# FFN modulation vectors: the partial sum is split into a rounded half and a remainder, and spread by two matmuls in the rounded format

## The chip, the core and the metric

The kernel runs on one core of a Trainium2 chip. The core has a matrix engine (TensorE, PE in the rows), a vector engine (VectorE, DVE), an engine for activations and copies (ScalarE, ACT), a general one (GpSimd, POOL) and a queue engine (SyncE, SP). They run side by side and meet only at semaphores. The metric is the device time of one execution in microseconds (us), lower is better; each version is timed in several runs and the median counts.

## What is computed

Two decoder layers on a sequence of 256 tokens with 1024 features. Each layer has two gated FFNs and a mixer between them, and a vector projected from the conditioning input `c` shifts, scales and gates each of them:

```
def reference(x, c, ada_w, ada_b, ...):
    h = x
    c_act = jax.nn.silu(c)
    for i in range(DEPTH):                                  # DEPTH = 2
        mod = c_act @ ada_w[i] + ada_b[i]                   # 1024 x 9216
        sh1, sc1, gt1, sh2, sc2, gt2, sh3, sc3, gt3 = jnp.split(mod, N_MOD, axis=-1)
        h = h + 0.5 * gt1 * swiglu(modulate(h, sh1, sc1), ffn_w_gu[i, 0], ffn_w_down[i, 0])
        u = modulate(h, sh2, sc2)
        m = dsa_mixer(u, ...) if i % 2 == 0 else rwkv7_mixer(u, ...)
        h = h + gt2 * m
        h = h + 0.5 * gt3 * swiglu(modulate(h, sh3, sc3), ffn_w_gu[i, 1], ffn_w_down[i, 1])
    return h
```

`swiglu(x, w_gu, w_down)` is `(silu(x @ gate) * (x @ up)) @ w_down` with 2816 hidden features. The change concerns `mod` alone, and of it the parts that are computed during the FFNs.

## The kernel before

**FFNs.** Every large matrix is used in two parts: a part rounded to the format fp32r (`_hi`, a copy on ACT) and the remainder (`_lo`, a subtraction on DVE). A product is then three matmuls, hi by hi, lo by hi and hi by lo (lines 662 to 664, whatever the matrices). There are four FFNs; I number them 0 to 3. Each runs 11 blocks of 256 hidden features (function `ffn` on each engine; `run_blocks` writes out the first three and the last ones and loops over the others). In block b PE does, in this order: gate and up products of the first 128 tokens (24 matmuls, `gate_up`), the transposes of the previous block's hidden values, the down products of the previous block for the first 128 tokens (12 matmuls, `down(ub - 1, 0)`), the gate and up products of the other 128 tokens, transposes, and `down(ub - 1, 1)`. The order on each engine is written by hand; nothing is scheduled. `down(ub - 1, 0)` waits for `split[2]`, the remainder of the down weights (DVE line 1506, `rest_of_down`), which itself waits for their rounding (ACT line 1112, `round_down`). That rounding waits for the end of `down(ub - 2, 1)`, since the rounded weights have one buffer. After the last block comes a tail in which both `down` calls stand together.

**Modulation vectors.** `mod` is made in 36 pieces of 512 columns, numbered v. Four are made at the start, three in the first mixer (DSA), the others in FFNs 0 to 2: 11, 11 and 7 pieces (`ADA_FFN`), one in each block while there are any. FFN 3 makes none. For a piece DVE does eight multiply-and-add steps over `ada_raw` (line 1433, `ada_products`), each 128x512, into `ada_acc`: this leaves 128 partial sums per column. These stand at the end of DVE's work for a block. In the next block PE sums them over the partitions, and at the same time spreads the sum to all 128 partitions, by one matmul with a matrix of ones in full fp32 (`ada_total`, line 635). It stands between the transposes and `down(ub - 1, 0)`. ACT copies the result to `mods` (line 1097). The weights come by DMAs that ACT issues (`load_ada`, lines 1087 and 1092), right behind `round_down` in its order.

ACT's order in a block from b = 1 on is: `silu` and `round_hidden` of the previous block, `round_down`, `load_ada`, `round_block` (two casts of the next gate and up weights, `gu_hi`), `silu`, `round_hidden`, `copy_mods`. DVE's is: `times_up`, `rest_of_hidden`, `rest_of_down`, `rest_of_block` (`gu_lo`), `times_up`, `rest_of_hidden`, `ada_products`. In the tail ACT does `silu`, `round_hidden(last, 0)`, `round_down`, `round_hidden(last, 1)`, and in FFNs 0 to 2 also the `round_block` of the next phase; DVE does `times_up`, `rest_of_hidden(last, 0)`, `rest_of_down`, `rest_of_hidden(last, 1)`, the next phase's `rest_of_block` and the residual. Each engine takes its instructions in order, so a wait holds all that stands behind it.

Of the kernel before, what the change touches and what calls it, by code (L numbers as in the profile page):

```python
# [5 lines left out]
P = 128  # L6
F32 = mybir.dt.float32
# [9 lines left out]
def trunk(nc, a, out):  # L17
# [37 lines left out]
    HALF = 512  # L55
# [9 lines left out]
    ON_PE = 2  # L65
    ADA_FFN = ((4, NB), (18, NB), (29, 7), (36, 0))

    ctx = ExitStack()
    with ctx:
# [67 lines left out]
        front_bias = place("front_bias", [P, ADA_FRONT, HALF], at=ada_at)  # L137
        front_acc = [ada_acc[:], hid[:].rearrange("p t c -> p (t c)")]
        c_wide = place("c_wide", [P, 2, P], at=spare_at)

# [81 lines left out]
        front_in = [[sem(f"front_in_{j}_{i}") for i in range(4)] for j in range(ADA_FRONT)]  # L222
        front_bias_in = sem("front_bias_in")
        front_step = sem("front_step")
        c_wide_ready = sem("c_wide_ready")
        ada_step = sem("ada_step")
        ada_sum = sem("ada_sum")
        mods_ready = sem("mods_ready")
        g_ready = [sem("g_ready_0"), sem("g_ready_1")]
# [184 lines left out]
        def _(sp):  # L414
# [3 lines left out]
            sp.dma_start(front_bias[0:1, :, :].rearrange("p v n -> p (v n)"), a["ada_b"][0:1, 0:ADA_FRONT * HALF]  # L418
                         ).then_inc(front_bias_in, 16)

# [210 lines left out]
        def _(pe):  # L631
# [14 lines left out]
            def front_total(j):  # L646

                pe.wait_ge(front_step, (j + 1) * (KD - ON_PE))
                nc.tensor.matmul(TB[j % 2][:], ones[:], front_acc[j % 2], start=False, stop=True).then_inc(ada_sum, 1)

            def turn_x(q, parts=range(4)):

                for i in parts:
                    pe.wait_ge(xn_ready, 4 * q + i + 1)
                    for k in range(4):
                        mm = nc.tensor.transpose(bank[4 + i][:, k * P:(k + 1) * P], xn[:, i % 2, k * P:(k + 1) * P],  # L656
                                                 ident[:])
                    mm.then_inc(xn_turned, 1)
# [55 lines left out]
            def ffn(f, q):  # L714
# [9 lines left out]
                def step(b, odd, ada):  # L724
# [6 lines left out]
                    if not (peeled and b == 0):  # L731
                        turn_hidden(ub - 1, 1, peeled and ub == 1)
                        if nv and not (peeled and b > nv):
                            pe.wait_ge(hT_ready[0], ub)
                            ada_total(v0 + b - 1, TB[0])
                        down(ub - 1, 0, peeled and b == 1, False)
                        pe.wait_ge(hid_ready[1], ub)
                    elif f:
                        pe.wait_ge(xT_ready, turned + 4)
# [14 lines left out]
                if nv == NB:  # L754
                    ada_total(v0 + NB - 1, TB[0])

# [310 lines left out]
            pe.wait_ge(consts, 5)  # L1067
            pe.wait_ge(c_wide_ready, 1)
            for j in range(3):
# [11 lines left out]
        def _(act):  # L1081
            def load_ada(v, layer, hv, first=False):
# [6 lines left out]
                for i in range(4):  # L1089
                    if not first:  # L1090
                        act.wait_ge(ada_step, done + 2 * i - 6)
                    act.dma_start(ada_raw[:, i], ada_w[layer, :, 2 * i:2 * i + 2, bass.ds(hv * HALF, HALF)]
                                  ).then_inc(ada_in[i], 16)

            def copy_mods(v, hv, spread):
# [254 lines left out]
            def ffn(f, q=None):  # L1350
# [30 lines left out]
                if f < 3:  # L1381

                    round_block(n0 + NB, (n0 + NB) % 2, width=DSA_SMALL if f == 0 else HALF)
                if nv == NB:
                    copy_mods(v0 + NB - 1, v0 % HV + NB - 1, TB[0])

            act.wait_ge(c_in, 16)
            nc.scalar.activation(cact[:], ccol[:], ACT.Silu).then_inc(c_ready, 1)
            nc.scalar.activation(c_wide[:], ccol[:, 0:ON_PE].unsqueeze(2).broadcast_to([P, ON_PE, P]), ACT.Silu
                                 ).then_inc(c_wide_ready, 1)  # L1390
            act.wait_ge(consts, 5)
            copy_mods(0, FRONT[0][0], TB[0])
            squares_of_h(0)
# [20 lines left out]
        def _(dve):  # L1414
# [55 lines left out]
            def first_modulate():  # L1470

                dve.wait_ge(front_bias_in, 16)
                front_products(0)
# [18 lines left out]
                rest_of_first_x(2)  # L1492
                rest_of_first_x(3)

            def rest_of_block(n, par, width=HALF, buf=raw, halves=range(2)):
# [246 lines left out]
            def ffn(f, q):  # L1742
# [194 lines left out]
```

## Time and profile before

| what | value |
|---|---|
| median of 3 runs | 1535.7 us (1533.28 to 1538.37) |
| the profiled execution | 1535.84 us, of which span 1534.1 us |
| PE matmul busy | 1297.3 us, 85% of the span |
| DVE busy | 957.4 us, 62% |
| ACT busy | 527.8 us, 34% |
| POOL busy | 79.3 us, 5% |
| the chain that ended last | PE 73%, DVE 16%, ACT 4%, DMA 3%, issue 2%, SP queue 2% |
| the same by line | lines 662, 664, 663: 19% each |
| `ada_total` (line 635) | 32.7 us busy, 64 records of 593 ns |
| `ada_products` (line 1433) | 168.4 and 23.8 us busy |

The time is the span plus 1.7 us around it. The program prints a line number per instruction; a helper such as `products` has one number for all its uses, so what tells the uses apart are the names of the tiles. The clock column is the TensorE clock that was granted, 1.00 for 2.4 GHz and 0.50 for 1.2 GHz. FFN 0 runs from about 42 to 257 us, FFN 1 from 471 to 683, FFN 2 from 687 to 900 and FFN 3 from 1326 to the end.

### The profile page before, as it was taken

The numbers are of one execution on the slowest core, as the hardware profiler recorded it, in microseconds if no ns is written. First come the engines' busy times: TensorE is split into PE (matmuls) and PEld (weight loads), VectorE is DVE, ScalarE is ACT, GpSimd is POOL, SyncE is SP. The second block draws the span as 40 slices with busy tenths as digits, with TensorE's granted clock in tenths as the row PEclk, the third lists the DMA queues.
The fourth block names the chain that finished last, engine by engine and source line by source line (L and its number), as shares of the span: only waits on it lengthen the run. The fifth ranks groups of instructions, "written<-read, shape, count | busy, mean of one in ns | idle before, by whom it ended". The sixth has DMA issues, their size and how long they took to land.

```text
span 1534.1 us, 16872 instructions
## 1 busy us (share of the span) xinstructions
PE 1297.3 (85%) x6370; PEld 1033.1 (67%) x6370; DVE 957.4 (62%) x1232; ACT 527.8 (34%) x694; POOL 79.3 (5%) x67
## 2 busy tenths in 40 slices
PE   5899996975988999979999938776746995899997
PEld 2678884763566888857788824675735994688885
DVE  6697776767457887768785364356592338645543
ACT  2433432353324333434443234343411011344331
POOL 1000000000000000000000000005260004000000
PEclk9899998885578999989999967888756555899998
DMA  9788874730017888668886442310102012455641
GB/s 315 281 297 286 278 253 162 254 129 1 0 60 256 297 303 289 224 214 270 296 303 208 79 127 91 115 56 0 28 0 56 2 56 91 137 184 167 208 146 55
DMA packets 186515, 252.19 MB, mean 164 GB/s; under 512 B 31506, under 2 KB 122642, under 8 KB 186450
## 3 DMA queue, kind: packets, MB, share of 16 engines
q1 hardware_dynamic: 151570, 184.14, 36.1%
q10 hardware_dynamic: 34880, 67.18, 12.7%
q8 instruction: 42, 0.69, 0.2%
q14 instruction: 23, 0.18, 0.0%
HBM read 249.19 MB, written 2.10 MB: 164 GB/s over the span
## 4 chain that ended last, share of the span: by engine, by line
PE 73%; DVE 16%; ACT 4%; DMA 3%; issue 2%; SPq 2%; ACTq 0%; POOL 0%; DVEq 0%; POOLq 0%
PE bank L662 19%; PE bank L664 19%; PE bank L663 19%; DVE inv_tmp L1670 2%; PE bank L814 2%; PE bank L635 2%; PE bank L1029 1%; PE bank L1037 1%; DVE gu_lo L1500 1%; PE bank L700 1%; PE bank L824 1%; DVE inv_out L1672 1%; PE bank L846 1%; PE bank L983 1%; DVE xn L1543 1%
## 5 line engine op out<-in xcount | busy, mean ns | idle before, releaser
L662 PE MATMUL bank<-gu_hi,xT_hi 128*128 128x512 f32 (+1 forms) x880 | 354.8, 403 | 17.0 <-ACT z L1169 8.4
L663 PE MATMUL bank<-gu_lo,xT_hi 128*128 128x512 f32 (+1 forms) x880 | 352.0, 400 | 0.0
L664 PE MATMUL bank<-gu_hi,xT_lo 128*128 128x512 f32 (+1 forms) x880 | 351.7, 400 | 0.0
L1500 DVE TENSOR_TENSOR gu_lo<-raw,gu_hi 128x2048 fp32r<-128x2048 f32 (+1 forms) x116 | 257.2, 2255 | 82.7 <-ACT gu_hi L1105 82.5
L1105 ACT CAST gu_hi<-raw 128x2048 fp32r<-128x2048 f32 (+1 forms) x116 | 213.3, 1883 | 82.0 <-PE bank L664 29.8
L662 PEld LDWEIGHTS bank<-gu_hi,xT_hi 128*128 128x128 f32 x880 | 172.9, 196 | 58.0 <-ACT z L1169 9.3
L663 PEld LDWEIGHTS bank<-gu_lo,xT_hi 128*128 128x128 f32 x880 | 172.8, 196 | 38.1 <-issue 1.0
L664 PEld LDWEIGHTS bank<-gu_hi,xT_lo 128*128 128x128 f32 x880 | 172.3, 196 | 36.1
L1506 DVE TENSOR_TENSOR dn_lo<-raw,dn_hi 128x2048 fp32r<-128x2048 f32 x44 | 100.8, 2291 | 123.2 <-ACT dn_hi L1112 123.2
L1433 DVE SCALAR_TENSOR_TENSOR ada_acc<-ada_raw,cact,ada_acc 128x512 f32<-128x512 f32 x224 | 168.4, 752 | 12.0 <-DVE ada_acc L1433 1.0
L662 PE MATMUL bank<-dn_hi,hT_hi 128*128 128x512 f32 x352 | 156.7, 445 | 17.9 <-DVE dn_lo L1506 17.9
L1119 ACT ACTIVATE hid<-bank 128x256 f32<-128x256 f32 x88 | 33.4, 381 | 317.9 <-PE bank L664 317.9
L664 PE MATMUL bank<-dn_hi,hT_lo 128*128 128x512 f32 x352 | 142.0, 403 | 0.0
L663 PE MATMUL bank<-dn_lo,hT_hi 128*128 128x512 f32 x352 | 141.6, 402 | 0.0
L1112 ACT CAST dn_hi<-raw 128x2048 fp32r<-128x2048 f32 x44 | 83.8, 1905 | 94.4 <-PE bank L664 94.4
L1511 DVE TENSOR_TENSOR hid<-hid,bank 128x256 f32<-128x256 f32 x88 | 36.6, 416 | 93.3 <-ACT hid L1119 93.3
L662 PEld LDWEIGHTS bank<-dn_hi,hT_hi 128*128 128x128 f32 x352 | 68.6, 195 | 38.6 <-issue 26.4
L663 PEld LDWEIGHTS bank<-dn_lo,hT_hi 128*128 128x128 f32 x352 | 68.7, 195 | 18.0 <-issue 5.7
L664 PEld LDWEIGHTS bank<-dn_hi,hT_lo 128*128 128x128 f32 x352 | 68.5, 195 | 15.7
L656 PE MATMUL bank<-ident,xn 128*128 128x128 f32 x96 | 24.7, 407 | 45.3 <-DVE xn L1543 44.1
L662 PE MATMUL bank<-xT_hi,gu_hi 128*128 128x256 f32 x128 | 38.7, 303 | 20.6 <-DVE xT_lo L1592 18.9
L656 PEld LDWEIGHTS bank<-ident,xn 128*128 128x128 f32 x96 | 16.0, 202 | 55.5 <-DVE xn L1543 53.0
(255 smaller groups left out, 1571.3 us busy)
## 6 DMA issues: line engine op xcount, KB each, us to landing
raw<-in_ffn_w_gu_dram SPq DMA_DIRECT2D x176, 512.0 KB, 6.3
ada_raw<-in_ada_w_dram ACTq DMA_DIRECT2D x128, 512.0 KB, 5.5
raw<-in_ffn_w_down_dram SPq DMA_DIRECT2D x44, 1024.0 KB, 6.9
raw<-in_rwkv_w_rkv_dram SPq DMA_DIRECT2D x24, 512.0 KB, 5.5
front<-in_ada_w_dram SPq DMA_DIRECT2D x16, 512.0 KB, 10.2
raw<-in_dsa_w_in_dram SPq DMA_DIRECT2D x16, 512.0 KB, 6.1
raw<-in_dsa_w_out_dram SPq DMA_DIRECT2D x8, 512.0 KB, 5.4
out_raw<-in_rwkv_w_out_dram SPq DMA_DIRECT2D x4, 512.0 KB, 5.4
```

Source lines behind the costliest of these rows:

```text
L635: nc.tensor.matmul(spread[:], ones[:], ada_acc[:], start=True, stop=True).then_inc(ada_sum, 1)
L656: mm = nc.tensor.transpose(bank[4 + i][:, k * P:(k + 1) * P], xn[:, i % 2, k * P:(k + 1) * P], ident[:])
L662: nc.tensor.matmul(out_ap, sta_hi, mov_hi, start=start, stop=False, skip_group_check=True)
L663: nc.tensor.matmul(out_ap, sta_hi, mov_lo, start=False, stop=False, skip_group_check=True)
L664: return nc.tensor.matmul(out_ap, sta_lo, mov_hi, start=False, stop=stop, skip_group_check=True)
L1105: nc.scalar.copy(gu_hi[:, par, 4 * i:4 * i + 4, 0:width], buf[:, i, 0:4 * width].rearrange("p (k c) -> p k c", k=4)).then_inc(hi_ready[i], 1)
L1112: nc.scalar.copy(dn_hi[:], raw[:, 2, :].rearrange("p (t d) -> p t d", t=2)).then_inc(hi_ready[2], 1)
L1119: nc.scalar.activation(hid[:, half, :], G[half][:, 0:FB], ACT.Silu).then_inc(silu_done[half], 1)
L1433: nc.vector.scalar_tensor_tensor(out=ada_acc[:], in0=ada_raw[:, k // 2, k % 2, :], scalar=cact[:, k:k + 1], in1=ada_acc[:] if k else ada_b ...
L1500: nc.vector.tensor_tensor(gu_lo[:, par, ks, 0:width], buf[:, i, 0:4 * width].rearrange("p (k c) -> p k c", k=4), gu_hi[:, par, ks, 0:width ...
L1506: nc.vector.tensor_tensor(dn_lo[:], raw[:, 2, :].rearrange("p (t d) -> p t d", t=2), dn_hi[:].bitcast(F32), ALU.subtract).then_inc(split[2 ...
L1511: nc.vector.tensor_tensor(hid[:, half, :], hid[:, half, :], G[half][:, FB:2 * FB], ALU.mult).then_inc(hid_ready[half], 1)
```

## The change

The change makes the sum over partitions in the rounded format too, in the FFNs alone. For each of the 29 pieces made in FFNs 0 to 2:

- ACT gets a copy `acc_hi` <- `ada_acc` that rounds to fp32r (`round_acc`), placed between `round_hidden` and `round_down`; it waits for the eighth product step.
- DVE gets a subtraction `acc_lo` <- `ada_acc` - `acc_hi` (`rest_of_acc`), between `rest_of_hidden` and `rest_of_down`; it waits for `acc_hi`.
- PE's fp32 matmul becomes two fp32r matmuls with rounded ones, over `acc_hi` and `acc_lo` (`ffn_total`), and waits for `acc_lo`.
- In the tails of FFNs 0 and 1 `round_acc` stands on ACT behind the next phase's `round_block`, while `rest_of_acc` stands on DVE ahead of `rest_of_down`.
- At the start ACT makes the rounded ones; the semaphores for `c` and for the first biases are joined, and so are those for what ACT makes of `c`. So ACT's first activation waits for the biases too.

The three pieces in DSA and the four at the start keep the fp32 matmul.

```
@@ PE
+            def ffn_total(f, b):
+                u = ADA_DONE[f] + b
+                pe.wait_ge(acc_ready, u + 1)
+                nc.tensor.matmul(TB[0][:], ones_r[:], acc_hi[:], start=True, stop=False)
+                nc.tensor.matmul(TB[0][:], ones_r[:], acc_lo[:], start=False, stop=True).then_inc(ada_sum, 1)
...
                             pe.wait_ge(hT_ready[0], ub)
-                            ada_total(v0 + b - 1, TB[0])
+                            ffn_total(f, b - 1)
...
@@ ACT
+            def round_acc(v):
+                act.wait_ge(ada_step, (v - ADA_FRONT) * KD + KD)
+                nc.scalar.copy(acc_hi[:], ada_acc[:]).then_inc(acc_hi_ready, 1)
...
                         round_hidden(ub - 1, 0, peeled and ub == 1)
+                        if nv and not (peeled and b > nv):
+                            round_acc(v0 + b - 1)
                         round_down(ub - 1, peeled and ub == 1)
...
                     round_block(n0 + NB, (n0 + NB) % 2, width=DSA_SMALL if f == 0 else HALF)
                 if nv == NB:
+                    round_acc(v0 + NB - 1)
                     copy_mods(v0 + NB - 1, v0 % HV + NB - 1, TB[0])
-            act.wait_ge(c_in, 16)
+            act.wait_ge(c_in, 2 * 16)
...
+            nc.scalar.copy(ones_r[:], ones[:]).then_inc(c_ready, 1)
...
@@ DVE
+            def rest_of_acc(f, b):
+                dve.wait_ge(acc_hi_ready, ADA_DONE[f] + b + 1)
+                nc.vector.tensor_tensor(acc_lo[:], ada_acc[:], acc_hi[:].bitcast(F32), ALU.subtract).then_inc(acc_ready, 1)
...
                         rest_of_hidden(ub - 1, 0)
+                        if nv and not (peeled and b > nv):
+                            rest_of_acc(f, b - 1)
                         rest_of_down(ub - 1)
...
                 rest_of_hidden(last, 0)
+                if nv == NB:
+                    rest_of_acc(f, NB - 1)
                 rest_of_down(last)
```

ACT's queue at the tail of FFN 1 and the start of FFN 2, after the change (`dn_hi` is the rounded down weights, `gu_hi` the rounded gate and up weights, `hT_hi` the rounded hidden values):

```order
L1127 CAST dn_hi<-raw 128x2048
L1140 CAST hT_hi<-bank 128x256
L1120 CAST gu_hi<-raw 128x2048 x2
L1108 CAST acc_hi<-ada_acc 128x512
L1112 COPY mods<-bank 128x512
```

Before, the same place had all of these but the `acc_hi` line, which now stands behind both `gu_hi` casts.

ACT's queue in block 1 of an FFN, after the change:

```order
L1140 CAST hT_hi<-bank 128x256
L1108 CAST acc_hi<-ada_acc 128x512
L1127 CAST dn_hi<-raw 128x2048
L1098 DMA ada_bias<-in_ada_b_dram 1x512
L1103 DMA ada_raw<-in_ada_w_dram 128x2x512 x4
L1120 CAST gu_hi<-raw 128x2048 x2
```

Here `acc_hi` came in ahead of `dn_hi`, so the down weights, the DMAs and the `gu_hi` casts all stand behind its wait.

## Rows read from the trace of the kernel before

**Rows 1.** Windows, two whole blocks of FFN 2: with a piece, and without one

```profile
core 0: us, PE busy (x) PEld busy (x) DVE busy (x) ACT busy (x) POOL busy (x), PEclk, DMA share, GB/s
779.80:797.60 17.80, 17.80 (x80) 14.24 (x79) 14.03 (x16) 7.29 (x8) 0.00 (x0) 1.00 0.85 294
831.10:848.05 16.95, 16.95 (x78) 13.87 (x77) 8.12 (x7) 6.78 (x7) 0.00 (x0) 1.00 0.57 186
```

**Rows 2.** Timeline of PE (start us, duration us, what), around one sum in FFN 0

```profile
158.65 1.02 PE L635 MATMUL bank<-ada_acc,ones 128*128 128x512 f32 x2
...
159.74 0.39 PE L663 MATMUL bank<-dn_lo,hT_hi 128*128 128x512 f32 x1
159.97 0.39 PE L664 MATMUL bank<-dn_hi,hT_lo 128*128 128x512 f32 x1
```

**Rows 3.** Timeline of ACT, then of DVE, one steady block of FFN 0

```profile
153.23 1.91 ACT L1112 CAST dn_hi<-raw 128x2048 fp32r<-128x2048 f32 x1 [2.42 <-PE bank L664]
...
171.02 1.90 ACT L1112 CAST dn_hi<-raw 128x2048 fp32r<-128x2048 f32 x1 [2.33 <-PE bank L664]
...
163.97 5.48 DVE L1433 SCALAR_TENSOR_TENSOR ada_acc<-ada_raw,cact,ada_acc 128x512 f32<-128x512 f32 x7
...
172.95 2.29 DVE L1506 TENSOR_TENSOR dn_lo<-raw,dn_hi 128x2048 fp32r<-128x2048 f32 x1 [2.83 <-ACT dn_hi L1112]
```

**Rows 4.** Timeline of ACT and DVE, one cast and one tensor operation of 128x512

```profile
263.86 0.58 ACT L1155 CAST xT_hi<-bank 128x512 fp32r<-128x512 f32 x1 [2.92 <-PE bank L656]
...
677.81 0.69 DVE L1561 TENSOR_TENSOR h<-h,xn 128x512 f32<-128x512 f32 x1
```

**Rows 5.** Timeline of ACT, DVE and PE, block 1 of FFN 0

```profile
59.60 1.90 ACT L1112 CAST dn_hi<-raw 128x2048 fp32r<-128x2048 f32 x1
...
60.78 4.82 DVE L1433 SCALAR_TENSOR_TENSOR ada_acc<-ada_raw,cact,ada_acc 128x512 f32<-128x512 f32 x6 [0.53 <-DVE ada_acc L1433]
...
66.19 2.28 DVE L1506 TENSOR_TENSOR dn_lo<-raw,dn_hi 128x2048 fp32r<-128x2048 f32 x1
...
66.41 1.04 PE L635 MATMUL bank<-ada_acc,ones 128*128 128x512 f32 x2
68.62 0.47 PE L662 MATMUL bank<-dn_hi,hT_hi 128*128 128x512 f32 x1 [1.17 <-DVE dn_lo L1506]
...
78.60 0.41 PE L700 MATMUL bank<-ident,hid 128*128 128x128 f32 x2 [1.53 <-issue]
```

**Rows 6.** Timeline of DVE and PE, block 1 of FFN 1

```profile
488.44 4.04 DVE L1433 SCALAR_TENSOR_TENSOR ada_acc<-ada_raw,cact,ada_acc 128x512 f32<-128x512 f32 x5
...
494.69 1.02 PE L635 MATMUL bank<-ada_acc,ones 128*128 128x512 f32 x2
495.49 0.47 PE L662 MATMUL bank<-dn_hi,hT_hi 128*128 128x512 f32 x1
```

**Rows 7.** Timeline of DVE and PE, block 1 of FFN 2

```profile
702.94 5.68 DVE L1433 SCALAR_TENSOR_TENSOR ada_acc<-ada_raw,cact,ada_acc 128x512 f32<-128x512 f32 x7
...
712.10 1.02 PE L635 MATMUL bank<-ada_acc,ones 128*128 128x512 f32 x2
```

**Rows 8.** Timeline of ACT and PE, tail of FFN 0

```profile
242.11 1.90 ACT L1112 CAST dn_hi<-raw 128x2048 fp32r<-128x2048 f32 x1 [2.33 <-PE bank L664]
...
244.18 0.77 ACT L1105 CAST gu_hi<-raw 128x288 fp32r<-128x288 f32 x2
...
246.48 0.47 PE L662 MATMUL bank<-dn_hi,hT_hi 128*128 128x512 f32 x1 [4.19 <-DVE dn_lo L1506]
```

**Rows 9.** Timeline of ACT, DVE and PE, tail of FFN 1

```profile
669.21 3.70 ACT L1105 CAST gu_hi<-raw 128x2048 fp32r<-128x2048 f32 x2
...
669.07 2.29 DVE L1506 TENSOR_TENSOR dn_lo<-raw,dn_hi 128x2048 fp32r<-128x2048 f32 x1 [3.73 <-ACT dn_hi L1112]
...
677.08 0.69 DVE L1559 SCALAR_TENSOR_TENSOR xn<-bank,mods 128x512 f32<-128x512 f32 x1 [0.99 <-PE bank L664]
...
671.51 0.77 PE L662 MATMUL bank<-dn_hi,hT_hi 128*128 128x512 f32 x1 [4.19 <-DVE dn_lo L1506]
```

**Rows 10.** Timeline of PE behind a pause, then the window that follows

```profile
35.33 0.47 PE L662 MATMUL bank<-gu_hi,xT_hi 128*128 128x512 f32 x1 [3.17 <-DVE gu_lo L1500]
...
35.90:45.80 9.90, 7.80 (x17) 4.93 (x16) 6.76 (x10) 2.38 (x2) 0.00 (x0) 0.50 0.33 106
```

More of the change, by code:

```diff
@@ L66, in trunk @@
     ADA_FFN = ((4, NB), (18, NB), (29, 7), (36, 0))
+    ADA_DONE = tuple(sum(n for _, n in ADA_FFN[:f]) for f in range(4))
     ctx = ExitStack()
@@ L114, in trunk @@
         chunk_decay = place("chunk_decay", [P, KD, NC])
+        ones_r = place("ones_r", [P, P], F32R, at=top["at"])
         rstat = place("rstat", [P, 128])
@@ L138, in trunk @@
         front_acc = [ada_acc[:], hid[:].rearrange("p t c -> p (t c)")]
+        acc_hi = place("acc_hi", [P, HALF], F32R, at=spare_at + 2048)
+        acc_lo = place("acc_lo", [P, HALF], F32R, at=spare_at + 4096)
         c_wide = place("c_wide", [P, 2, P], at=spare_at)
@@ L222, in trunk @@
         front_in = [[sem(f"front_in_{j}_{i}") for i in range(4)] for j in range(ADA_FRONT)]
-        front_bias_in = sem("front_bias_in")
         front_step = sem("front_step")
-        c_wide_ready = sem("c_wide_ready")
         ada_step = sem("ada_step")
         ada_sum = sem("ada_sum")
+        acc_hi_ready = sem("acc_hi_ready")
+        acc_ready = sem("acc_ready")
         mods_ready = sem("mods_ready")
@@ L418, in _ @@
             sp.dma_start(front_bias[0:1, :, :].rearrange("p v n -> p (v n)"), a["ada_b"][0:1, 0:ADA_FRONT * HALF]
-                         ).then_inc(front_bias_in, 16)
+                         ).then_inc(c_in, 16)
             def load_front(j):
@@ L754, in ffn @@
                 if nv == NB:
-                    ada_total(v0 + NB - 1, TB[0])
+                    ffn_total(f, NB - 1)
             def dsa(q):
@@ L1067, in _ @@
             pe.wait_ge(consts, 5)
-            pe.wait_ge(c_wide_ready, 1)
+            pe.wait_ge(c_ready, 3)
             for j in range(3):
@@ L1384, in ffn @@
                 if nv == NB:
+                    round_acc(v0 + NB - 1)
                     copy_mods(v0 + NB - 1, v0 % HV + NB - 1, TB[0])
[L1387 removed]
+            act.wait_ge(c_in, 2 * 16)
             nc.scalar.activation(cact[:], ccol[:], ACT.Silu).then_inc(c_ready, 1)
             nc.scalar.activation(c_wide[:], ccol[:, 0:ON_PE].unsqueeze(2).broadcast_to([P, ON_PE, P]), ACT.Silu
[L1390 removed]
+                                 ).then_inc(c_ready, 1)
             act.wait_ge(consts, 5)
+            nc.scalar.copy(ones_r[:], ones[:]).then_inc(c_ready, 1)
             copy_mods(0, FRONT[0][0], TB[0])
@@ L1470, in first_modulate @@
             def first_modulate():
-                dve.wait_ge(front_bias_in, 16)
+                dve.wait_ge(c_in, 2 * 16)
                 front_products(0)
```

## The prediction

> **What bounds the kernel now.** I read the windows of single blocks first, then the timelines of PE, ACT and DVE side by side where the change puts something. In a block that makes a piece of `mod`, PE is busy for all 17.80 us at full clock, while DVE is busy for 14.03, ACT for 7.29 and the DMA engines 0.85 of the time; in a block without a piece PE is again busy throughout, for 16.95 us [rows 1]. So in the FFN blocks PE sets the pace, and what PE is spared there counts in full, as long as the other engines keep up. At the ends of the FFNs it is different: PE waits 4.19 us there for the remainder of the down weights [rows 8, 9], and in block 1 of FFN 0 it waits 1.17 us for it [rows 5]. There a later `dn_lo` counts in full. The change touches both kinds of place.
>
> **Part 1, the cheaper sum, in steady blocks.** Matmuls of 128x512 in the rounded format follow each other 0.23 us apart (159.74 to 159.97). The record of the first down matmul is stretched, so I count back: the one that starts at 159.74 is the second of its group, its predecessor took a slot from about 159.51, and the fp32 sum had PE from 158.65 to there, 0.86 us [rows 2]. The two windows say the same: 17.80 less 16.95 is 0.85 [rows 1]. Two rounded matmuls are 2 x 0.23 = 0.46, so a block gets 0.40 us shorter. The price in the other direction is certain within little: at best the new pair costs less by a few hundredths, at worst the switch of operands shows and 0.05 is lost.
>
> Do the others keep up? The new cast on ACT needs about 0.58 us and the subtraction on DVE about 0.69 [rows 4]. ACT waits for PE for 2.33 us ahead of `dn_hi` at 171.02. The products end at 163.97 + 5.48 = 169.45, `acc_hi` then takes ACT to about 170.1, nearly a microsecond before it is wanted for `dn_hi`. DVE waits 2.83 us for `dn_hi` [rows 3] and does `acc_lo` inside that. So both are hidden. The ring that could take over is: `dn_hi` starts at 153.23, products end at 169.45, 16.22 us later [rows 3]; with the cast 0.58 and two hand-overs of some 0.05 it is 16.9, against a block of 17.80 - 0.40 = 17.40. PE still sets the pace, by 0.5 us. The DMA share would go from 0.85 to 0.87 [rows 1].
>
> This holds for blocks 2 to 10 of FFNs 0 and 1 and blocks 2 to 7 of FFN 2: 9 + 9 + 6 = 24 blocks, **-9.6 us** (24 x 0.40; bounds -8.4 and -10.6).
>
> **Part 2, block 1 of an FFN.** Here the products are late against ACT, because block 0 has no down work. In FFN 0 ACT started `dn_hi` at 59.60, but the products ended only at 60.78 + 4.82 = 65.60. Now ACT stands at `round_acc` until then: `acc_hi` to 66.2, `dn_hi` (1.90) to 68.1, `dn_lo` (2.28) to 70.4, and `down(0, 0)` starts at about 70.5 and not at 68.62 [rows 5], 1.9 later. Behind it PE used to wait 1.53 us at 78.60 [rows 5], which swallows most: the delay left is 1.9 - 1.5 = 0.4 us. That cover holds if the late ada DMAs behind the cast do no harm. They are issued some 5 us later, which leaves the gate and up weights more of the bandwidth; I see no loss. But PE now stands idle from the end of the sum, about 67.3 with the wait for `acc_lo`, to 70.5: 3.2 us. After a pause of 3.17 us at the start of the program the clock was at 0.50 for the next 9.9 us, after the pauses of 1.17 and 1.53 it was not [rows 10, 5]. What a fall costs: in the tail of FFN 1, behind a pause of 4.19 us, twelve down matmuls took 677.08 - 671.51 = 5.6 us, where twelve at full clock take 2.8; 2.8 lost [rows 9]. At the edge as this pause is, I take a bit more than half of that, 1.6. Term: **+2.0 us** (bounds +0.3 and, from half of the 9.9 us of low clock, +5).
>
> The Trainium skill, "TensorE: Matmul & The Clock Gate", section "HAM oscillation — how this bites in real kernels", has it that a wait between two bursts of matmuls sends the engine back to half rate, so that the burst behind starts cold. By that rule this term is about 2.0; without it, 0.4. The pauses of 3.17 us [rows 10] and 4.19 us [rows 9] agree with it.
>
> In FFN 1 the products end at 488.44 + 4.04 = 492.48. `acc_hi` to 493.1, `dn_hi` to 495.0, `dn_lo` to 497.3: `down` starts at 497.4 against 495.49 [rows 6], and nothing behind it waits. The pause is 495.15 to 497.4, 2.2 us, between rows that kept the clock and a row that lost it; I take it as kept. **+1.9 us** (bounds +1.4 and, with a lost clock, +4.7).
>
> In FFN 2 the products end at 702.94 + 5.68 = 708.62; the same steps give 713.5 for the end of `dn_lo`, while the fp32 sum at 712.10 ended at 712.96 [rows 7]. **+0.5 us** (bounds +0.2 and +1.0). In all three ACT's `gu_hi` gets 1.6 to 2.4 us later as well; PE wants the following `hid` some 7 us after that, so it is covered.
>
> **Part 3, the tails.** In the tail DVE stops at `rest_of_acc` until ACT has made `acc_hi`, and ACT does that only after `hT_hi` and the two `gu_hi` casts of the next phase. In FFN 0 these are narrow: 244.18 + 0.77 = 244.95, `acc_hi` to 245.5, `acc_lo` to 246.15. `dn_lo`, which began right behind `dn_hi` at 244.0, begins at 246.2, and PE starts at 248.6 instead of 246.48 [rows 8]: **+2.2 us** (bounds +2.0 and +4.0, the upper one if the low clock lasts longer over the two `down` calls). In FFN 1 they are full size: 669.21 + 3.70 = 672.9, `acc_hi` to 673.5, `acc_lo` to 674.1, so `dn_lo` starts 5.1 us later than at 669.07 and PE at 676.6 instead of 671.51. The residual at 677.08 waits for that `down` [rows 9] and moves with it: **+5.0 us** (bounds +4.2 and +5.5). The cheaper sums of the tails save nothing, as PE idles for microseconds behind them.
>
> **Part 4, the start.** ACT's first activation now waits for the bias DMA and for one more small cast. The first product waits for weights that land much later. 0.
>
> **Sum.** -9.6 + 2.0 + 1.9 + 0.5 + 2.2 + 5.0 = **+2.0 us**. The profiled execution, 1535.84 us with 1534.1 of span and 1.7 around it, becomes 1537.8; it stands 0.1 above the median, so I predict **1537.7 us**, which is 0.13% more and no change that can be told: about 0.3% (4.6 us) is what a measurement of this kernel can tell from none.
>
> **Rivals.**
> *(a) The clock stays up in block 1 of FFN 0 and the tails overlap a little better.* The pause of 3.2 us is so close to the one row of 3.17 that it may go either way; then part 2 begins with +0.4, the tails cost 2.0 and 4.4. Sum -9.6 + 0.4 + 1.9 + 0.5 + 2.0 + 4.4 = -0.4: **1535.3 us**. Chance 0.22.
> *(b) Slower: the pauses cost clock everywhere.* If block 1 of FFN 0 and block 1 of FFN 1 both lose the 2.8 us of [rows 9] (0.4 + 2.8 = 3.2 and 1.9 + 2.8 = 4.7), and the longer pause lengthens the tail of FFN 0 to 3.9, the sum is -9.6 + 3.2 + 4.7 + 0.5 + 3.9 + 5.0 = +7.7: **1543.4 us**. It decides at a pause of between 1.53 us, which kept the clock [rows 5], and 3.17 us, which lost it [rows 10]. Chance 0.20.
> *(c) Slower: the ring of ACT and DVE takes over.* If the cast and its hand-overs take 1.2 us instead of 0.7, the ring of 16.9 reaches 17.4; at 1.4 it would take 0.2 us back in each of 24 blocks, +4.9: **1542.6 us**. Against it: every hand-over from DVE to ACT and back seen in the rows takes under 0.1 us. Chance 0.05.
> *(d) Faster: the waits of part 3 do not appear,* because ACT gets to `acc_hi` sooner than its order says. Then -9.6 + 2.0 + 1.9 + 0.5 = -5.2: **1530.5 us**. The order on ACT is fixed, so only 0.05.
> The forecast has the remaining 0.48.
>
> **How the numbers follow.** The forecast and rival (a) hold 0.70; to leave out no more than 0.2 the range must go into (b) and (c), and ends at the price of (b). Downwards it takes in (a) with the better bound of part 1 and of block 1 of FFN 1, -0.4 - 1.0 - 0.5 = -1.9, and the 2 us by which single runs differ: 1532. Range **1532 to 1543.5**. Faster by over 0.3% (under 1531.1): (d) and a sliver of (a), 0.07. Slower by over 0.3% (over 1540.3): (b), (c) and the upper end of the forecast, 0.27. Within: 0.66.
>
> **What the profile after would show.** Part 1: blocks 17.4 us apart in the steady part (starts of `dn_lo`), PE without idle time, ACT still waiting for PE ahead of `dn_hi`. Part 2: in block 1 of each FFN an `acc_hi` that starts as the eighth product ends, `dn_hi` behind it, and PE idle ahead of the first down matmul for 3.2, 2.2 and 1.0 us; the clock in the stretch behind tells (a) from the forecast and from (b). Part 3: PE idle in the tails of FFNs 0 and 1 for 6.3 and 9.3 us and not 4.19, DVE waiting for ACT's `acc_hi`; FFN 2 and FFN 3 end as before. The prediction is wrong if steady blocks are 17.6 or longer (a bound that I don't see) or if the idle time of the tails has not grown.

## The result, and the profile after

| | kernel before | kernel after |
|---|---|---|
| median of its runs | 1536.82 us (20 runs, 1533.28 to 1538.37) | 1539.19 us (20 runs, 1536.09 to 1542.13) |
| ratio, 95% interval | | 1.0017 [1.001, 1.0024] |
| profiled execution: span | 1534.1 us | 1537.0 us |
| granted clock, mean | 0.845 | 0.840 |

The change costs 0.17%, some 2.6 us. The interval leaves out 1, so by this many runs the kernel is a little slower. It stays within the 0.3% that the prediction called no change. The median of before has moved from 1535.7 (3 runs) to 1536.82 (20 runs), so 1.1 of the 1.5 us between the 1537.7 predicted and 1539.19 are the starting point and not the change.

The page after says little by itself; busy time per engine and the chain that ended last:

```profile
PE 1283.5 (84%) x6370; PEld 1033.1 (67%) x6370; DVE 977.6 (64%) x1261; ACT 545.4 (35%) x724; POOL 78.5 (5%) x67
...
PE 69%; DVE 18%; ACT 4%; DMA 4%; issue 2%; SPq 2%; ACTq 0%; POOL 0%; DVEq 0%; POOLq 0%
```

PE is most of the chain, and DVE the second. Where they take turns is seen only place by place.

**A steady block.** The window of one whole block of FFN 2 with a piece (columns as in [rows 1]), then the timeline of PE around a sum in FFN 1:

```profile
779.80:797.16 17.36, 17.36 (x80) 14.23 (x79) 14.72 (x17) 7.91 (x9) 0.00 (x0) 1.00 0.88 303
```

```profile
603.34 0.38 PE L711 MATMUL bank<-ident,hid 128*128 128x128 f32 x2
603.47 0.47 PE L659 MATMUL bank<-acc_hi,ones_r 128*128 128x512 f32 x1
603.79 0.40 PE L660 MATMUL bank<-acc_lo,ones_r 128*128 128x512 f32 x1
604.02 0.39 PE L673 MATMUL bank<-dn_hi,hT_hi 128*128 128x512 f32 x1
```

A block takes 17.36 us and not 17.80 [rows 1], 0.44 less, with PE busy in all of it. The four rows of the sum show why: the record at 603.47 is stretched over its predecessor, so I count back one slot of 0.23 from 603.79 to about 603.56; from there to the first down matmul at 604.02 the pair takes 0.46 us, where the fp32 sum took 0.86 [rows 2]. The other engines have 0.69 us (DVE, 14.03 to 14.72) and 0.62 us (ACT, 7.29 to 7.91) more to do.

What ACT and DVE do in such a block of FFN 1:

```profile
580.77 1.91 ACT L1127 CAST dn_hi<-raw 128x2048 fp32r<-128x2048 f32 x1 [0.40 <-PE bank L675]
...
597.12 0.62 ACT L1108 CAST acc_hi<-ada_acc 128x512 fp32r<-128x512 f32 x1 [1.32 <-DVE ada_acc L1452]
598.13 1.90 ACT L1127 CAST dn_hi<-raw 128x2048 fp32r<-128x2048 f32 x1 [0.38 <-PE bank L675]
...
582.71 2.29 DVE L1530 TENSOR_TENSOR dn_lo<-raw,dn_hi 128x2048 fp32r<-128x2048 f32 x1 [1.61 <-ACT dn_hi L1127]
...
591.61 5.48 DVE L1452 SCALAR_TENSOR_TENSOR ada_acc<-ada_raw,cact,ada_acc 128x512 f32<-128x512 f32 x7
```

ACT waits 1.32 us for the eighth product, casts for 0.62, and then still waits 0.38 us for PE ahead of `dn_hi`, where it had waited 2.33 [rows 3]. So ACT comes to the down weights with 0.38 us in hand. DVE waits 1.61 us for `dn_hi`, before 2.83 [rows 3].

**Block 1 of FFN 0**, timeline of ACT, DVE and PE:

```profile
67.20 0.62 ACT L1108 CAST acc_hi<-ada_acc 128x512 fp32r<-128x512 f32 x1 [5.68 <-DVE ada_acc L1452]
67.72 1.90 ACT L1127 CAST dn_hi<-raw 128x2048 fp32r<-128x2048 f32 x1
69.54 3.71 ACT L1120 CAST gu_hi<-raw 128x2048 fp32r<-128x2048 f32 x2
...
62.34 4.82 DVE L1452 SCALAR_TENSOR_TENSOR ada_acc<-ada_raw,cact,ada_acc 128x512 f32<-128x512 f32 x6 [0.53 <-DVE ada_acc L1452]
...
69.66 2.29 DVE L1530 TENSOR_TENSOR dn_lo<-raw,dn_hi 128x2048 fp32r<-128x2048 f32 x1 [1.11 <-ACT dn_hi L1127]
...
72.09 0.47 PE L673 MATMUL bank<-dn_hi,hT_hi 128*128 128x512 f32 x1 [2.53 <-DVE dn_lo L1530]
```

ACT stands for 5.68 us at the cast, until the products end at 62.34 + 4.82 = 67.16, and all that is behind it in its queue stands with it. PE's pause ahead of its first down matmul has grown from 1.17 [rows 5] to 2.53 us. In the profile before, the second half of the weights of block 2 was rounded here, after a wait for its DMA:

```profile
73.94 1.91 ACT L1105 CAST gu_hi<-raw 128x2048 fp32r<-128x2048 f32 x1 [5.92 <-DMA raw<-in_ffn_w_gu_dram]
```

After, both halves run at 69.54 without a wait. The clock behind PE's pause, and behind the pause of 1.86 us in block 1 of FFN 1 (windows, the columns as before; the clock is the third number from the end):

```profile
72.80:76.10 3.30, 3.30 (x9) 2.53 (x9) 3.30 (x2) 1.47 (x4) 0.00 (x0) 0.50 1.05 396
...
500.00:503.40 3.40, 3.40 (x16) 2.77 (x15) 3.40 (x2) 1.97 (x4) 0.00 (x0) 1.00 1.08 331
```

In FFN 0 the clock fell to 0.50, which is 1.2 GHz of the 2.4, for 3.3 us: 9 matmul records where 16 stand in a like window at full clock. In FFN 1 it stayed at 1.00. The first down matmul of block 1 in FFN 1 and in FFN 2, each with PE's pause ahead of it:

```profile
499.72 0.47 PE L673 MATMUL bank<-dn_hi,hT_hi 128*128 128x512 f32 x1 [1.86 <-DVE dn_lo L1530]
...
717.71 0.47 PE L673 MATMUL bank<-dn_hi,hT_hi 128*128 128x512 f32 x1 [1.44 <-DVE dn_lo L1530]
```

**The tails.** Timeline of PE in the tail of FFN 0, then of ACT, DVE and PE in the tail of FFN 1:

```profile
247.87 0.76 PE L673 MATMUL bank<-dn_hi,hT_hi 128*128 128x512 f32 x1 [6.24 <-DVE dn_lo L1530]
```

```profile
667.51 1.90 ACT L1127 CAST dn_hi<-raw 128x2048 fp32r<-128x2048 f32 x1 [2.33 <-PE bank L675]
...
669.58 3.70 ACT L1120 CAST gu_hi<-raw 128x2048 fp32r<-128x2048 f32 x2
673.18 0.62 ACT L1108 CAST acc_hi<-ada_acc 128x512 fp32r<-128x512 f32 x1
...
673.83 0.69 DVE L1517 TENSOR_TENSOR acc_lo<-ada_acc,acc_hi 128x512 fp32r<-128x512 f32 x1 [8.12 <-ACT acc_hi L1108]
674.44 2.28 DVE L1530 TENSOR_TENSOR dn_lo<-raw,dn_hi 128x2048 fp32r<-128x2048 f32 x1
...
676.87 0.76 PE L673 MATMUL bank<-dn_hi,hT_hi 128*128 128x512 f32 x1 [9.17 <-DVE dn_lo L1530]
```

`dn_hi` is done at 669.4, but `dn_lo` starts only at 674.44, because DVE stands for 8.12 us at `acc_lo`, whose operand `acc_hi` ACT makes behind both `gu_hi` casts. PE waits 9.17 us and not 4.19 [rows 9]. In FFN 0, where those casts are narrow, it waits 6.24 and not 4.19 [rows 8].

**The stages set side by side.** The intervals leave out what lies ahead of them. They run from the first down matmul of block 1 to that of the tail, in us of the profiled executions:

| | before | after | change |
|---|---|---|---|
| FFN 0 | 177.86 | 175.78 | -2.08 |
| FFN 1 | 176.02 | 177.15 | +1.13 |
| FFN 2 | 173.76 | 170.84 | -2.92 |

In FFN 1 the +1.13 is the pause of the tail, 9.17 - 4.19 = +4.98, against nine blocks: 9 x 0.43 = -3.9. In FFN 2 there is no tail piece, and six blocks give 6 x 0.43 = -2.6; the other 0.3 us are not accounted for. In FFN 0 nine blocks give -3.9, the pause of the tail +2.05, the lost clock about +1.4, and the pause of 1.53 us in block 2 [rows 5] is gone: together -2.0.

### The profile page after: what moved, and what is told of

Its sections match the earlier page's. It is cut to its first block, busy times and chain, and to the rows that moved or that the text cites. A ratio compares the mean times of both kernels' runs of the same rounds, so it can differ in the third digit from the quotient of the medians.

```text
span 1537.0 us, 16951 instructions
## 1 busy us (share of the span) xinstructions
PE 1283.5 (84%) x6370; PEld 1033.1 (67%) x6370; DVE 977.6 (64%) x1261; ACT 545.4 (35%) x724; POOL 78.5 (5%) x67
## 4 chain that ended last, share of the span: by engine, by line
PE 69%; DVE 18%; ACT 4%; DMA 4%; issue 2%; SPq 2%; ACTq 0%; POOL 0%; DVEq 0%; POOLq 0%
PE bank L673 18%; PE bank L675 17%; PE bank L674 17%; DVE inv_tmp L1694 2%; DVE gu_lo L1524 2%; PE bank L825 2%; DVE ada_acc L1452 2%; PE bank L1040 1%; ACT gu_hi L1120 1%; PE bank L1048 1%; PE bank L711 1%; PE bank L835 1%; DVE dn_lo L1530 1%; DVE inv_out L1696 1%; PE bank L857 1%
## 5 line engine op out<-in xcount | busy, mean ns | idle before, releaser
L673 PE MATMUL bank<-dn_hi,hT_hi 128*128 128x512 f32 x352 | 147.0, 418 | 29.6 <-DVE dn_lo L1530 29.6
```

Of the source, the lines that this page charges most:

```text
L673: nc.tensor.matmul(out_ap, sta_hi, mov_hi, start=start, stop=False, skip_group_check=True)
```

## The experiments

All eight kernels are the kernel after with the new form of the sum given to some of the pieces alone, or put elsewhere in the queues. A small helper `is_split(b)` says which pieces b of an FFN have the new form; the others keep `ada_total`, the fp32 matmul. "First" is the piece summed in block 1 of an FFN (3 of them), "middle" the 24 of the steady blocks, "last" the two of the tails of FFNs 0 and 1. The first four kernels ran together on one chip, the last four together on another; ratios are to the kernel before on the same chip, and kernels of different groups are compared by them. The half width of their intervals, 0.0009 to 0.0014, is 1.4 to 2.2 us.

### No sum in the new form

```
-    ffn_total(f, b - 1)
+    ffn_total(f, b - 1) if is_split(b - 1) else ada_total(v0 + b - 1, TB[0])
...
-    if nv and not (peeled and b > nv):
+    if nv and not (peeled and b > nv) and is_split(b - 1):
         round_acc(v0 + b - 1)
```

with `is_split` false for all pieces. What is left of the change is the start: the rounded ones and the joined semaphores.

> The changed kernel with all 29 sums of the FFNs put back to the fp32 matmul over ada_acc; of the change only the edits at the start are left (joined semaphores, ACT's first activation waits for the biases, one cast of ones). Theory: the start costs nothing, ratio to the kernel before 1.000 within 0.1%. Rival: the start edits shift something in the first 60 us; in the changed kernel's trace the first transpose of hidden values in FFN 0 stood at 60.4 us and in the kernel before at 58.9. If the edits do that, it is at 60.4 here too and the time is 1.5 us (0.1%) longer; if it is scatter between runs, its place differs from profile to profile of kernels with the same start.

Measured: 1537.2 us (11 runs), ratio 1.0007 [0.9998, 1.0016]. The start costs nothing that can be told. The profile of this kernel reads in FFN 1 as that of before, 176.03 us from the first down matmul to that of the tail, against 176.02. Its FFN 0 began at another time than before, though: the first transpose of hidden values at 59.40 and not at 58.86. Over the ten profiles of this study that time lies between 57.4 and 60.4, in no order that goes by the edits. A comparison of absolute times between two profiles is therefore uncertain by some microseconds from FFN 0's start, and I compare intervals. The pause of 1.53 us in block 2 of FFN 0 [rows 5] is not in this profile either, although the sums are those of before: its `gu_hi` waited 2.76 us for the DMA and not 5.92.

### The middle pieces alone

`is_split` true for the 24 pieces of the steady blocks.

> The two-matmul sum only where PE sets the pace: pieces made in blocks 1 and later and summed in blocks 2 to 10 of FFNs 0 and 1 and 2 to 7 of FFN 2, 24 sums. The first piece of each FFN and the last of FFNs 0 and 1 keep the fp32 matmul. Theory: 24 x 0.42 = 10 us less than before (ratio 0.9935), steady blocks 17.37 us apart, PE idle in the tails 4.19 us as before and 1.2 us in block 1 of FFN 0. Rival (ACT and DVE lose something in each block as well): clearly less than 10 us gained.

Measured: 1526.69 us (6 runs), ratio 0.9944 [0.9933, 0.9956]. Against the kernel with no new sum that is -10.5 us by the medians, 0.44 a block (-9.7 us by the ratios, uncertain by 2.2). PE in the tails of FFNs 0 and 1 has its old waits, here that of FFN 1:

```profile
665.00 0.77 PE L686 MATMUL bank<-dn_hi,hT_hi 128*128 128x512 f32 x1 [4.19 <-DVE dn_lo L1544]
```

FFN 1 takes 172.24 us, 3.78 less than before, nine times 0.42. The gain of the cheaper sum is there in full.

### First and middle pieces

> As the run with 24 sums, plus the first piece of each of FFNs 0 to 2, summed in block 1; the last pieces of FFNs 0 and 1 stay fp32. Theory: block 1 gives back 1.5 to 2.0 us in FFN 0, 1.9 in FFN 1 and 0.6 in FFN 2, together some 4.2, so 5.8 us less than before (ratio 0.9962). Rival (the whole loss of the changed kernel sits in the tails): as fast as the run with 24 sums, 0.9935.

Measured: 1532.29 us (10 runs), ratio 0.9975 [0.9966, 0.9984]. The three first pieces cost 1532.29 - 1526.69 = +5.6 us by the medians, 4.8 by the ratios; expected were 4.2. PE's waits ahead of the first down matmul of FFNs 0, 1 and 2:

```profile
70.26 0.77 PE L686 MATMUL bank<-dn_hi,hT_hi 128*128 128x512 f32 x1 [2.69 <-DVE dn_lo L1544]
...
497.93 0.47 PE L686 MATMUL bank<-dn_hi,hT_hi 128*128 128x512 f32 x1 [2.51 <-DVE dn_lo L1544]
...
710.95 0.47 PE L686 MATMUL bank<-dn_hi,hT_hi 128*128 128x512 f32 x1 [1.31 <-DVE dn_lo L1544]
```

and the clock in the windows behind the first two:

```profile
70.50:73.80 3.30, 3.30 (x10) 2.60 (x11) 3.30 (x2) 1.93 (x4) 0.00 (x0) 0.61 1.06 391
498.10:501.50 3.40, 3.40 (x16) 2.76 (x16) 3.40 (x2) 2.08 (x4) 0.00 (x0) 1.00 1.06 398
```

The clock fell behind 2.69 us (0.61 is the mean of a window that holds both levels) and stayed at 1.00 behind 2.51.

### Middle and last pieces

> As the run with 24 sums, plus the last piece of FFNs 0 and 1, with the cast where the change has it, behind the casts of the next phase on ACT. Theory: the tails give back 2.2 and 4.0 to 5.0 us, so 3 to 4 us less than before (ratio 0.9977), PE idle 6.3 and 9.2 us in the two tails. Rival (tails cost nothing, since what follows waits anyway): 0.9935.

Measured: 1536.25 us (12 runs), ratio 0.9998 [0.9988, 1.0008]. Against the middle pieces alone the two tail pieces cost +9.6 us, where 6.2 to 7.2 were expected. The pauses of the tails are to the hundredth those of the kernel after, 6.24 and 9.17 us, which is 2.05 + 4.98 = 7.0 us. The other 2.6 us are not in these pauses. By the ratios the two kernels differ by 0.0054, or 8.3 us, uncertain by 2.3, so what goes beyond 7.0 is not clear of the noise.

The two profiled executions lie further apart than the medians, 11.4 us. Up to the tail of FFN 0 this kernel issues the same instructions as the one with the middle pieces alone, yet it reaches that point 2.3 us later in its profile (240.65 against 238.32, the starts of PE's pauses). The rows that differ are in block 2 of FFN 0, timelines of ACT and PE of the kernel with middle and last pieces:

```profile
73.84 1.91 ACT L1133 CAST gu_hi<-raw 128x2048 fp32r<-128x2048 f32 x1 [4.97 <-DMA raw<-in_ffn_w_gu_dram]
...
78.51 0.64 PE L724 MATMUL bank<-ident,hid 128*128 128x128 f32 x2 [2.48 <-issue]
```

and of ACT in the kernel with the middle pieces alone, which has no such pause of PE:

```profile
71.51 1.91 ACT L1133 CAST gu_hi<-raw 128x2048 fp32r<-128x2048 f32 x1 [2.75 <-DMA raw<-in_ffn_w_gu_dram]
```

The gate and up weights of block 2 landed 2.3 us later, with the same DMAs issued. In this stretch the DMA engines are full (share 1.05 in the window of before from 72.80 to 76.10), and when each transfer lands differs from one execution to the next. That is 2.3 of the 11.4 us between the two profiles, and the pauses are 7.0; the last 2.1 came behind the first down matmul in the tail of FFN 1 and are not accounted for. Whether late weights also stand behind the 2.6 us between the medians is open. The kernel with middle and last pieces and the early cast, below, speaks against it: its profile has the same late weights (6.05 us of waiting), and its ratio is as low as that of the middle pieces alone (0.9936 and 0.9944).

### The cast of the tail put ahead

```
                 round_hidden(last, 0)
+                if nv == NB and is_split(NB - 1):
+                    round_acc(v0 + NB - 1)
                 round_down(last, False)
...
                 if nv == NB:
-                    round_acc(v0 + NB - 1)
                     copy_mods(v0 + NB - 1, v0 % HV + NB - 1, TB[0])
```

All 29 pieces have the new form.

> The changed kernel with one thing moved: in the tails of FFNs 0 and 1 ACT's cast acc_hi stands ahead of the rounding of the down weights, and not behind the next phase's casts. All 29 sums stay in the new form. Theory (the place of that cast is what the tails cost): PE's idle time in the two tails is 4.19 us again, and the time falls by the tails' 7 to 9 us, to that of the run with the first and middle pieces: ratio 0.997 to 0.998 against before. Rival (the added work in the tail costs by itself, wherever it stands): as the changed kernel, 1.0017.

Measured: 1531.57 us (7 runs), ratio 0.997 [0.9959, 0.9981]. ACT and PE in the tail of FFN 1:

```profile
662.55 0.63 ACT L1121 CAST acc_hi<-ada_acc 128x512 fp32r<-128x512 f32 x1
...
664.99 1.90 ACT L1140 CAST dn_hi<-raw 128x2048 fp32r<-128x2048 f32 x1 [1.81 <-PE bank L688]
...
669.36 0.77 PE L686 MATMUL bank<-dn_hi,hT_hi 128*128 128x512 f32 x1 [4.19 <-DVE dn_lo L1544]
```

The cast moved into time in which ACT waits for PE anyway (1.81 us are still left of the wait), and PE's pause is 4.19 us again, as before the change. Between the ratios of the kernel after and of this one lie 1.0017 - 0.997 = 0.0047, or 7.2 us, uncertain by 2: the term of the tails in the prediction, 2.2 + 5.0, undone by one moved line.

### Middle and last pieces, with the cast of the tail put ahead

`is_split` false for the first piece of each FFN, the cast of the tail as above.

> As the run with middle and last pieces, with the same cast moved ahead in the tails; the first piece of each FFN stays fp32. 26 sums in the new form. Theory: the last pieces then cost and bring nothing, so the same as the run with 24 sums: ratio 0.9944, within 0.1%. Rival as above: up to 1.000, what the run with the late cast had.

Measured: 1526.94 us (5 runs), ratio 0.9936 [0.9922, 0.9949]. This is faster than the kernel before and the kernel after: 26 of the 29 sums in the new form, each where it costs nothing. It is no faster than the 24 middle ones alone (0.9944, the intervals overlap), as expected, because behind the sum of a tail PE idles for microseconds (8.04 and 6.78 us here). Against the kernel with all 29, on the same chip, it gives 1531.57 - 1526.94 = 4.6 us for the three first pieces, 5.2 by the ratios.

It differs from the kernel with middle and last pieces in the place of the cast alone, so it is a second pair for that one line: 0.9998 - 0.9936 = 0.0062, or 9.5 us, uncertain by 2.6. Both pairs agree with the 7.0 us of the pauses within their noise.

### All pieces, with the first sum behind the down matmuls

Can the three first pieces be had for nothing too? In block 1 the sum was put behind half of the down work on PE, the cast on ACT behind the rounding of the down weights and the ada DMAs, the subtraction behind `dn_lo` on DVE:

```
 # PE, block 1
-                            ffn_total(f, b - 1)
                         down(ub - 1, 0, peeled and b == 1, False)
+                        if nv and peeled and b == 1:
+                            ffn_total(f, 0)
...
 # ACT, block 1: behind load_ada
+                    if nv and peeled and b == 1:
+                        round_acc(v0)
...
 # DVE, block 1
                         rest_of_down(ub - 1)
+                        if nv and peeled and b == 1:
+                            rest_of_acc(f, 0)
```

> All 29 sums in the new form, cast early in the tails, and in block 1 of each FFN everything of the sum moved behind the down weights: ACT's cast behind the rounding of the down weights and the DMAs that it issues, DVE's remainder behind theirs, PE's two matmuls behind the first down products. Theory: block 1 no longer waits for dn_lo longer than before, so 27 sums of 0.42 us are saved: about 11.3 us less than the kernel with the start edits alone, ratio 0.993 to 0.9945. Rival (block 1 also pays for work moved onto ACT and DVE there): no better or slightly slower than the run with 24 sums, 0.995 or more.

Measured: 1528.34 us (5 runs), ratio 0.9956 [0.9943, 0.997]. The theory missed, and the rival's figure came. It is not better than the kernel with 26 pieces (1526.94); the intervals overlap. The order of the queues did what it should in FFNs 1 and 2 (PE's pause in block 1 of FFN 1 is 0.90 us), but in FFN 0 there are two pauses; timelines of ACT and PE:

```profile
74.40 1.91 ACT L1136 CAST gu_hi<-raw 128x2048 fp32r<-128x2048 f32 x1 [4.17 <-DMA raw<-in_ffn_w_gu_dram]
...
68.72 0.77 PE L686 MATMUL bank<-dn_hi,hT_hi 128*128 128x512 f32 x1 [2.19 <-DVE dn_lo L1549]
...
90.61 0.47 PE L686 MATMUL bank<-dn_hi,hT_hi 128*128 128x512 f32 x1 [2.06 <-DVE dn_lo L1549]
```

The first pause is the old one: DVE starts `dn_lo` only behind its products, at 66.29, as before at 66.19 [rows 5]. Before, the fp32 sum filled 0.86 us of PE's time there and 1.17 us of pause were left; with the sum moved away all of it is pause, 2.19 us, and the clock behind it fell to 0.51. The second comes from late weights: they wait for their DMA again, 4.17 us, so DVE's products of block 2, and `acc_hi`, `dn_hi` and `dn_lo` behind them, are late too (ACT waits 5.82 us for those products).

In the kernel after the weights of block 2 did not wait: there ACT's queue held the ada DMAs back behind the cast, and `gu_hi` ran at 69.54 with no wait, for both halves. The DMA engines had next to nothing to do meanwhile (share 0.04 from 65.60 to 68.00, against 1.06 in the same window of before). All three profiles in which the first cast blocks ACT's queue (after, first and middle, cast of the tail put ahead) have no such wait; all seven others have one, of 2.75 to 6.05 us. The blocked queue cost PE its pause of 2.53 us and gave it the weights of block 2 in time.

### A wider cast, for the margin of the ring

The kernel with the middle pieces alone, and ACT's cast three times as wide:

```
-        acc_hi = place("acc_hi", [P, HALF], F32R, at=spare_at + 2048)
+        acc_wide = place("acc_wide", [P, 3, HALF], F32R, at=spare_at)
+        acc_hi = acc_wide[:, 0, :]
...
-    nc.scalar.copy(acc_hi[:], ada_acc[:])
+    nc.scalar.copy(acc_wide[:], ada_acc[:].unsqueeze(1).broadcast_to([P, 3, HALF]))
```

> The run with 24 sums, with ACT's cast three times as wide (it writes acc_hi and two more copies, 128x1536), so some 1.6 us and not 0.62. It measures the margin of the ring ACT, DVE, ACT in a steady block. From the changed kernel's rows the ring is 16.26 us from the start of dn_hi to the start of acc_hi, plus the cast: 16.8 to 16.9 against a block of 17.36. Theory: at 1.0 us more the ring is 17.8 to 17.9 and takes over, blocks 17.9 apart, which costs 0.5 in each of the 24 blocks, 12 us: about the time of before or a little more, ratio 1.001 to 1.003. Rival (other slack hides the cast, since ACT is busy only 41% of a block): blocks stay 17.36 apart, ratio 0.9944.

Measured: 1530.52 us (5 runs), ratio 0.9968 [0.9954, 0.9982]. The blocks did not grow: the first down matmuls of the steady blocks lie 17.36 or 17.37 us apart, as with the narrow cast, and in the window of such a block of FFN 1 PE is busy throughout. That window, then ACT:

```profile
580.00:597.36 17.36, 17.36 (x79) 14.22 (x79) 14.81 (x17) 8.68 (x9) 0.00 (x0) 1.00 0.88 302
```

```profile
577.80 1.90 ACT L1141 CAST dn_hi<-raw 128x2048 fp32r<-128x2048 f32 x1
580.39 3.72 ACT L1134 CAST gu_hi<-raw 128x2048 fp32r<-128x2048 f32 x2 [0.69 <-issue]
...
593.70 1.48 ACT L1122 CAST acc_wide<-ada_acc 128x1536 fp32r<-128x1536 f32 x1 [1.32 <-DVE ada_acc L1467]
595.08 1.90 ACT L1141 CAST dn_hi<-raw 128x2048 fp32r<-128x2048 f32 x1
```

ACT has no wait for PE left ahead of `dn_hi`, and still PE sets the pace. From `dn_hi` to the end of the products it took 577.80 to 593.70 = 15.9 us and not the 16.22 of [rows 3]. A part of the 16.22 was itself a wait, ahead of `gu_hi`; in the kernel after it was 1.14 us:

```profile
583.81 3.72 ACT L1120 CAST gu_hi<-raw 128x2048 fp32r<-128x2048 f32 x2 [1.14 <-issue]
```

The profile names no releaser for it. In both rows the cast starts 0.13 us behind the last of the ada DMAs that ACT issues. With the wide cast the wait is 0.69 us, 0.45 less. My expectation of 17.9 us blocks came from adding the cast to a sum with slack in it. The margin of the ring was more than what I had put it at: a cast of 1.48 us, 0.86 us more than one of 0.62, does not lengthen a block. Where the limit lies was not measured.

The +3.8 us against the narrow cast (by the ratios +3.7, uncertain by 2.8) are not in the steady blocks. In the profiles the tail of FFN 0 comes 2.6 us later (245.12 against 242.51), and FFN 1 takes as long as with the narrow cast (172.47 against 172.24). In FFN 0 PE paused 2.29 us at 77.93 and 1.57 at 90.33. The former is the late landing of weights seen above; whether the wider cast adds to the latter is open.

## Why the prediction was right, step by step

**The span.** Predicted +0.13%, measured +0.17% [0.1, 0.24]. The mechanism holds in its parts as well: a gain in the steady blocks, a loss in block 1 and a larger one in the tails. That the total comes within 0.04% of the measured one is in part luck, since single terms are off by about 1 us and each is known to some 2 us only.

**Part 1, the steady blocks.** Predicted -0.40 a block and -9.6 us; measured -0.44 in the windows, and between the kernels with and without the 24 sums -10.5 us by the medians and -9.7 by the ratios. The count back over stretched records was right, 0.46 us for the pair. Period and waits said what they should: ACT still waits 0.38 us for PE, DVE 1.61 us for ACT.

**Part 2, block 1.** Predicted +2.0, +1.9 and +0.5, together 4.4 us; measured 5.6 and 4.6 us (by the ratios 4.8 and 5.2) in the two pairs of kernels that differ in it. In FFN 0 the pause is 2.53 us where I had 3.2. The steps on ACT and DVE took what I gave them (products end at 67.16, `dn_lo` at 71.95, 4.8 us later), but PE's sum ended at 72.09 - 2.53 = 69.56, 2.4 us behind the products and not 1.7. PE was itself late there: its gate and up products ran at a clock of 0.50 until 65.6, around a pause of 7.29 us that ended at 60.42, ahead of the first transpose of hidden values; before, that pause was 4.42 us, ended at 58.86, and the clock was back by 63. That start differs between profiles without regard to the edits, so the shorter pause is in part luck. The clock fell all the same, for 3.3 us, and 9 records in place of 16 say that about 7/16 of that, 1.4 us, was lost; predicted 1.6. In the kernel with the cast of the tail put ahead, whose block 1 is the same, it was low for 5.6 us behind a pause of 2.69, so this price scatters as well. The pause of 1.53 us at 78.60 [rows 5], which was to swallow part of the delay, is gone. But I took it for a fixed part of the kernel before, and it isn't one: the kernel with no new sum does not have it. The reason that I only touched is the larger one: the weights of block 2 no longer wait for their DMA at all (5.92 us of waiting before), because the ada DMAs stand behind the cast. In FFN 1 the first down matmul comes 1.9 us later, counted from PE's wait at the turn into that FFN (which moved by 2.35 us against before, the matmul by 4.23), as predicted; its pause is 1.86 us where I had 2.2 and kept the clock. In FFN 2 the same difference is 1.0 us (4.14 and 5.15) where I had 0.5, and the pause 1.44 us where I had 1.0: this term was half its size.

By the Trainium skill, "TensorE: Matmul & The Clock Gate", section "HAM oscillation — how this bites in real kernels", the burst behind a wait starts at half rate; the waits of its example are longer than those here. The window of FFN 0 agrees (0.50 behind 2.53 us). That of FFN 1 shows that not each wait does it (1.00 behind 1.86 us).

**Part 3, the tails.** Predicted pauses 6.3 and 9.3 us, measured 6.24 and 9.17, and DVE waits for ACT's cast as drawn (8.12 us in FFN 1). Of the price, 2.2 + 5.0 = 7.2 us, the moved cast gave back 7.2 in one pair of kernels and 9.5 in the other. The 9.6 us between the middle pieces alone and middle with last ones are 2.6 us more than the two pauses, which is not clear of the noise. Not all of a longer pause need reach the end: from the first down matmul of the tail of FFN 1 to the first transposes of FFN 2 the kernel after took 14.52 us and the one before 15.74, a stretch that takes 14.35 to 15.46 us in the other profiles.

**Part 4, the start.** 0; measured 1.0007 [0.9998, 1.0016].

**The rivals.** (a), the clock stays up: no, it fell in FFN 0. (b), it falls everywhere: no, FFN 1 kept it. (c), the ring takes over: no, ACT had 0.38 us to spare ahead of `dn_hi`, and by the wide cast the ring had more. (d), the tails' waits do not appear: no, but the 1530.5 us worked out for it is close to what moving the cast gave (1531.57). Its price was about right, the kernel it was for was another.

**Do the terms add up?** The single terms from the medians (-10.5 + 5.6 + 9.6 = +4.7, from the kernel with no new sum at 1.0007) make 1.0038 and not 1.0017. By the ratios it is 0.9975 + 0.9998 - 0.9944 = 1.0029, and the gap of 0.0012 is within the noise of the four ratios taken together (0.0019). So a dependence between first and last pieces isn't shown. One is conceivable: with the first piece in the new form the ada DMAs are held back and late weights in FFN 0 cost nothing.

## What to carry to other kernels

A cheaper operation on the bounding engine is worth its saving only where its new inputs are made in time that was idle: here 24 of 29 places gave 10.5 us and the other five took back more than that, some 13 us. On an engine that works in order, look at what the new instruction stands behind (two casts, 3.70 us together, for one of 0.62 us, in the tail) and at what stands behind it, DMAs included; one line moved returned 7.2 us. And before adding to a ring of engines, subtract the waits that it already holds: a measured length of a ring is an upper bound of its work.

## What the runs showed of the hardware

Which pause costs TensorE its clock is not told by its length alone. Pauses of PE, and the mean granted clock in the 3 us behind them (the levels are 1.00 and 0.50; a mean in between is a window that holds both):

| pause, us | where | clock behind |
|---|---|---|
| 1.86 | after, FFN 1, block 1 | 1.00 |
| 2.05 | middle and last, cast ahead, at 77.85 | 0.56 |
| 2.06 | all moved, at 90.61 | 1.00 |
| 2.19 | all moved, at 68.72 | 0.51 |
| 2.29 | wide cast, at 77.93 | 0.53 |
| 2.48 | middle and last, at 78.51 | 0.50 |
| 2.51 | first and middle, FFN 1 | 1.00 |
| 2.53 | after, FFN 0 | 0.50 |
| 2.69 | first and middle, FFN 0 | 0.61 |
| 2.69 | cast of the tail put ahead, FFN 0, at 71.09 | 0.50 |

The clearest pair is 2.05 and 2.51 us; windows of the kernel with 26 pieces behind the former, and of the one with all pieces moved behind its two:

```profile
78.20:81.50 3.30, 3.30 (x10) 2.57 (x10) 3.02 (x5) 0.37 (x1) 0.00 (x0) 0.56 0.87 248
```

```profile
68.90:72.10 3.20, 3.20 (x8) 2.53 (x9) 2.11 (x2) 1.33 (x1) 0.00 (x0) 0.51 1.07 379
90.80:94.10 3.30, 3.30 (x15) 2.70 (x15) 3.30 (x2) 2.06 (x4) 0.00 (x0) 1.00 1.08 400
```

The low level lasted some 3 to 3.5 us behind most of the pauses that lost it and 5.6 us behind that at 71.09. All pauses above 1.86 us in this table that stand in FFN 0 before 80 us lost the clock; what differs for the other two is left open.

The second thing is how much a start fed by DMA scatters. Four kernels here issue the same work up to block 2 of FFN 0 (middle alone, middle and last, the same with the cast ahead, and but for the cast's width the wide one): their gate and up weights waited 2.75, 4.97, 6.05 and 5.35 us for the DMA, and PE paused 0, 2.48, 2.05 and 2.29 us for it. A change of 2 us in this place can't be read from one profile. Nor can it in the first mixer, where nothing was changed: from its first transposes to those of FFN 1 the ten profiles take 208.0 to 211.1 us, in no order that goes by the edits.
